# The decayed state of a chunked RWKV-7 scan computed on VectorE in place of ScalarE

## What is computed

```
S_t = S_{t-1} diag(decay_t) + (S_{t-1} a_t) b_t^T + v_t k_t^T
y_t = S_t r_t
```

## Time and profile before

| what | value |
|---|---|
| median of 3 runs | 2883.16 us (2877.56 to 2883.21) |
| profiled execution, its own time | 2883.16 us |
| span from its first to its last instruction | 2881.4 us |
| mean granted TensorE clock | 0.97 of full |
| PE busy | 2717.5 us, 94% |
| DVE busy | 1306.1 us, 45% |
| ACT busy | 851.3 us, 30% |
| POOL busy | 786.1 us, 27% |

### The profile page before, as it was taken

How to read it: one execution, slowest core, us unless ns; L and a number is a source line. 1 busy time by engine, 2 the same in 40 slices (tenths; PEclk the granted TensorE clock), 3 DMA queues, 4 the chain that set the end, 5 groups by cost and what they waited for, 6 DMA issues and landing times.

```text
span 2881.4 us, 43450 instructions
## 1 busy us (share of the span) xinstructions
PE 2717.5 (94%) x17968; PEld 2183.6 (76%) x17968; DVE 1306.1 (45%) x2210; ACT 851.3 (30%) x1727; POOL 786.1 (27%) x439
## 2 busy tenths in 40 slices
PE   6999999996899999999898999999998998899999
PEld 5787878775767767676777888788886877777777
DVE  4225243426837356383531433544444005476753
ACT  3434444444133231322212211211113114255531
POOL 1222222211221221211344132233322444332332
PEclk9999999998999999999998999999999997999999
DMA  3111111111101010111432211111111130111122
GB/s 123 41 45 41 52 41 52 41 37 37 35 23 49 27 48 28 34 45 60 153 114 66 73 44 45 43 44 44 44 49 38 46 110 15 41 41 38 45 89 95
DMA packets 200901, 153.97 MB, mean 53 GB/s; under 512 B 5120, under 2 KB 183680, under 8 KB 200064
## 3 DMA queue, kind: packets, MB, share of 16 engines
q1 hardware_dynamic: 186256, 106.44, 12.5%
q10 hardware_dynamic: 14448, 44.74, 4.0%
HBM read 128.10 MB, written 23.07 MB: 52 GB/s over the span
## 4 chain that ended last, share of the span: by engine, by line
PE 78%; DVE 15%; ACT 5%; issue 1%; DMA 1%; ACTq 0%; DVEq 0%; SPq 0%
PE gemm L515 21%; PE gemm L517 19%; PE gemm L516 19%; ACT prob L1933 2%; DVE neg_logits L1475 2%; DVE prob L1490 1%; PE scores L566 1%; PE scores L757 1%; PE weighted L593 1%; PE weighted L817 1%; PE probs_t L754 1%; PE probs_t L578 1%; PE scores L892 1%; PE scores L746 1%; DVE stats L1479 1%
## 5 line engine op out<-in xcount | busy, mean ns | idle before, releaser
L515 PE MATMUL gemm<-h_hi,w_hi 128*128 128x512 f32 x1936 | 798.2, 412 | 9.7 <-ACT q_t L1689 7.6
L517 PE MATMUL gemm<-h_hi,w_lo 128*128 128x512 f32 x1936 | 760.7, 393 | 0.0
L516 PE MATMUL gemm<-h_lo,w_hi 128*128 128x512 f32 x1936 | 759.7, 392 | 0.0
L483 POOL CAST w_hi<-w_raw 128x1024 fp32r<-128x1024 f32 (+1 forms) x188 | 195.2, 1038 | 2017.0 <-PE gemm L517 1973.7
L484 POOL TENSOR_TENSOR w_lo<-w_raw,w_hi 128x1024 fp32r<-128x1024 f32 (+1 forms) x188 | 457.6, 2434 | 15.0
L515 PEld LDWEIGHTS gemm<-h_hi,w_hi 128*128 128x128 f32 x1936 | 366.1, 189 | 102.3 <-issue 22.9
L517 PEld LDWEIGHTS gemm<-h_hi,w_lo 128*128 128x128 f32 x1936 | 365.9, 189 | 79.9
L516 PEld LDWEIGHTS gemm<-h_lo,w_hi 128*128 128x128 f32 x1936 | 366.8, 189 | 66.6 <-issue 1.9
L1369 DVE TENSOR_TENSOR scaled_product<-gemm,norm_rstd 128x512 f32<-128x512 f32 x116 | 80.2, 692 | 334.3 <-PE gemm L517 326.0
L515 PE MATMUL gemm<-xn_hi,w_hi 128*128 128x512 f32 x320 | 135.1, 422 | 3.4 <-DVE scaled_product L1369 2.0
L1094 DVE CUSTOM_DVE_ANT_0 neg_logits<-scores,bias_tile 128x128 f32<-128x128 f32 (+1 forms) x192 | 67.6, 352 | 150.1 <-PE scores L566 144.3
(11 more groups left out here) (424 smaller groups left out, 4308.5 us busy)
## 6 DMA issues: line engine op xcount, KB each, us to landing
w_raw<-in_w_in SPq DMA_DIRECT2D x73, 512.0 KB, 3.9
w_raw<-in_a_w_in SPq DMA_DIRECT2D x48, 512.0 KB, 3.7
gates_scratch<-o_f ACTq DMA_DIRECT2D x32, 256.0 KB, 2.0
merge_gates<-gates_scratch ACTq DMA_DIRECT2D x4, 2048.0 KB, 15.2
w_raw<-in_a_w_out SPq DMA_DIRECT2D x16, 512.0 KB, 3.3
w_raw<-in_b_w_in SPq DMA_DIRECT2D x16, 512.0 KB, 3.8
x_rows<-in_x SPq DMA_DIRECT2D x8, 512.0 KB, 8.3
w_raw<-in_w_out SPq DMA_DIRECT2D x8, 512.0 KB, 3.4
```

What stands on the lines that cost most here:

```text
L483: Q(pool.tensor_copy(hi, raw[:, s, 0:nk, :]))
L515: pe.matmul(G[b][:], whi[:, s, k, :], hi(k, h), start=first, stop=False)
L516: pe.matmul(G[b][:], whi[:, s, k, :], lo(k, h), start=False, stop=False)
L517: m = pe.matmul(G[b][:], wlo[:, s, k, :], hi(k, h), start=False, stop=last)
```

## The change

The two instructions that make `se` go from ScalarE to VectorE. There they stand behind the copy to `xs` and ahead of the wait for TensorE's second group, and nothing signals or waits for `state_decayed` any more, since VectorE both writes and reads `se`. They are also run for the last chunk, where nothing reads the result. On ScalarE the call of `side_out` for a chunk's first place moves from behind the wait and copy of L1787 to ahead of them.

```diff
@@ VectorE
                     V(v.tensor_copy(xs[:], PV[:, 0:C]), E("sx_sb"))
+                    for hh, r in enumerate(rows2):
+                        V(v.tensor_scalar(se[r, :], SV[r, hh, 0, c, :], e_end[r, c:c + 1], None, ALU.mult))
                     dve.wait_ge(E("su_full"), n + 1)
                     V(v.tensor_copy(SV[lo_, 0, 1, c, :], MB[lo_, 0:C]), E("su_even"))
                     if c < NCH - 1:
                         dve.wait_ge(E("ss_full"), 15 * p + c + 1)
-                        dve.wait_ge(E("state_decayed"), 15 * p + c + 1)
@@ ScalarE
                 for c in range(NCH):
-                    if c < NCH - 1:
-                        act.wait_ge(E("state"), NCH * p + c + 1)
-                        A(a.activation(se[lo_, :], SV[lo_, 0, 0, c, :], ACT.Copy, scale=e_end[lo_, c:c + 1]))
-                        A(a.activation(se[hi_, :], SV[hi_, 1, 0, c, :], ACT.Copy, scale=e_end[hi_, c:c + 1]), E("state_decayed"))
+                    side_out(p, f"scan{3 * c}")
                     act.wait_ge(E("su_full"), NCH * p + c + 1)
                     A(a.activation(SV[hi_, 1, 1, c, :], MB[hi_, 0:C], ACT.Copy), E("su_odd"))
-                    side_out(p, f"scan{3 * c}")
                     side_out(p, f"scan{3 * c + 1}")
```

## The result

The changed kernel takes 2909.02 us (median of four runs, of which three lie between 2904.11 and 2909.05) against 2880.36 us for the kernel before over the four runs made with it. The ratio is 1.0099, 95% interval 1.0081 to 1.0118: slower by about 28.5 us. (The fourth run, with a mean granted clock of 0.669, is left out of the ratio.) The forecast was +19.15 us, 2902.3 us, and its range ended at 2907: the direction and the cause of the stalls were right, but the growth was 9 us more than forecast, and the range missed the time by 2 us. That last distance is within the scatter: with six more runs of the changed kernel there are nine to go by, between 2901.89 and 2912.30 us, with a median of 2907.7. The growth, 28.5 us against 19.15, is the firmer measure of what was missed.

A forecast was written before the change was run, and what follows sets the result against it. TensorE was taken to bound the scans. From 2883.16 us, -0.42 (stall gone) + 2.40 (moved `side_out`) + 17.17 (decays held by GpSimd) = +19.15 gave 2902.3 us, +0.66%, range 2888 to 2907.

The forecast's parts named there:

- What bounds the scan: In the scans TensorE, busy 72.58 of 73 us in pair 1's, sets the end; the other engines have time.
- -0.42 for the stall that goes: Pair 0, chunk 4: without the decays ScalarE's copy is no longer late for L780, saving 0.42 us.
- +2.40 for the moved `side_out`: In eight chunks the moved call delays ScalarE's copy L1787 and so TensorE's L780, +2.40 us in all.
- The 0.02 us of the three chunks 13: Chunk 13, z half: the moved call makes L780 0.02 us late, three times.
- Decays at rest: Undisturbed decays on VectorE take 0.26 us each, hidden under filler step and second group, cost 0.
- +17.17 for the decays held by GpSimd: Chunks 4, 10 of pair 0 and 4, 7, 11 of pairs 1, 2: decays wait for GpSimd's instructions, +17.17 us.
- No collision: Rival: the decays on VectorE don't need what GpSimd holds; 2885.1 us, no change; chance 0.08.
- the second decay slips in: Rival: VectorE's second decay runs between GpSimd's two instructions; +5.8 us, 2889.0 us; chance 0.12.
- ScalarE was the hidden bound: Rival: the decays' leaving ScalarE shortens every chunk, up to -42 us; chance 0.02.
- These stalls cost in full: At TensorE's L780 the stalls behind held decays count at their own length, +17.17 us, with nothing added for half clock.
- a rival with a chance of 0.06: TensorE's long stalls also bring half clock, 1.7 us more for each of four: +26 us, 2909 us; chance 0.06.

The follow-up runs named there:

- decay_psum: The changed kernel with each decay made a SCALAR_TENSOR_TENSOR that adds a zeroed strip of PSUM; ratio 1.0021 to the kernel before.
- side_only: The kernel before with only `side_out` of the first place moved ahead of L1787's wait, decays staying on ScalarE; ratio 1.0016.
- stall_long: The kernel before with VectorE clearing a strip of PSUM 7 or 6 times ahead of L1297's copy in four chunks; ratio 1.0062.

## Why the prediction was right, and where it fell short

- **What bounds the scan.** Right. ScalarE's 41 us of freed time shortened nothing but chunk 4 of pair 0. decay_psum, which frees ScalarE too, has no scan that gained from it beyond that.
- **-0.42 for the stall that goes.** Right: in decay_psum L780 of chunk 4 in pair 0 starts 0.44 us sooner and has no wait.
- **+2.40 for the moved `side_out`.** Right in five chunks (side_only: L780 2.3 us late in all, scans +2.1). The 0.02 us of the three chunks 13 didn't come.
- **Decays at rest, 0.26 us, hidden.** Right: 246 to 255 ns, and L1299 still starts at 1.61.
- **+17.17 for the decays held by GpSimd.** Right in all eight chunks that it lists (its last part lists the same eight and calls them seven), and in the seven where GpSimd had a next instruction the second decay lost to it. Against its usual place in an undisturbed chunk L780 is 16.8 us late behind held decays (1.75 and 1.09, then twice 1.40, 2.82 and 2.75), where 17.17 were forecast. *No collision* and *the second decay slips in* are refuted by the 15 long instructions; *ScalarE was the hidden bound* by decay_psum.
- **The clock.** This is the step that failed. The forecast's sum ended with the stalls, "These stalls cost in full, since TensorE waits in order and no slack follows", and so put the half clock behind them at nothing, leaving it to a rival with a chance of 0.06, at +26 us and 2909 us. That rival came true. The sum as I made it holds for the stalls (18.7 us against 19.15), and 9.8 us of half clock come on top in the profiled run, 8.4 of them behind the stalls. stall_long shows that long stalls alone do it. That the rival's 2909 is the measured time is partly luck: it started from 2883.16 where the median of the kernel before is 2880.36, and it had 6.8 us of half clock in place of 9.8.
- **Why it was put so low.** I argued from a stretch of preparation, busy 9.82 of 12 us at clock 1.00. TensorE's idle time there is one piece of 2.18 us, while the new long stalls leave it idle for 2.68 and 2.75 us in one piece. And the kernel before has falls of its own that I passed over, in the preparation of pair 1 and in that of pair 0, in the columns of the earlier trace rows:

```profile
854.00:957.00 103.00, 96.06 (x1356) 80.34 (x1354) 77.69 (x90) 28.28 (x40) 17.59 (x8) 0.98 0.13 40
...
753.00:777.00 24.00, 18.72 (x484) 17.55 (x484) 19.77 (x20) 2.50 (x6) 5.86 (x3) 0.93 0.09 25
```

In the first the clock is at half for 3.4 us, behind the same idle piece of 2.18 us that pairs 2 and 3 have without a fall. In the second TensorE is idle for 3.29 us in one piece from 759.30, and at half clock from 762.66 to 766.07. So this part of the trace of before had three idle pieces of 2.18 us, one of them with a fall behind it, and one of 3.29, longer than the new ones, with a fall as well. I argued from one of the two without a fall, and the rival deserved far more than 0.06. With a third for it the range would have reached 2909.

## What to carry to other kernels

Moving an instruction to an engine with idle time isn't free because its own duration fits the gap: look at which memories it reads and writes and what another engine is doing to them at that moment, and read the max, not the median, of a like instruction. A stall of 2.7 us or more on TensorE is priced with the half clock that may follow it, here about half of the stall again; how likely it is can be counted in the trace of the kernel as it stands, from its idle pieces with and without a fall behind them. And a long instruction of an engine off the critical path can be worth cutting in pieces when others are held for its whole length: that gave 1.2 to 1.4% here, from an engine that was never the bound.

## What the runs showed of the hardware

- A held pair of small VectorE instructions waits for GpSimd's present instruction and then for its next as well, although both are ready in between: first 2392 and then 2386 ns for 64 elements in chunk 7 of pair 1. In the change this happened in all seven pairs that met two GpSimd instructions in a row (none slipped in), with starts that the profile puts at the same hundredth of a us.
- Four stalls of 3.5 us (14.2 in all) dropped the granted clock to half behind them, sixteen of 0.9 to 1.2 us (15.0 in all) did not: 0.94 and 1.00 over the scans. In between it is a matter of chance: idle pieces of 2.65 to 2.75 us had a fall 10 times of 12, those of 2.15 to 2.19 us 9 times of 21.
- The cost of cutting GpSimd's instructions is real but was hidden: L484 takes 2.43 us on the mean whole, 1.33 for a half and 0.78 for a quarter.
